# A two-layer encoder trunk on one core: how the fetched rows' sums are added, where the fetch dots stand, and the order of work at the layer border

## Chip, cores and metric

The kernel runs on one core of a Trainium2 chip, in one launch for both layers. The metric is the device time in microseconds (us); the median of three runs of the kernel before is 2080.5 us (2078.16 to 2082.45). One execution of it was also taken by the profiler: all rows below come from that one.

## What is computed

256 tokens of width 1024 go through two layers, float32 throughout. Cut to what matters here:

```python
def reference(x, ...):
    for layer in range(DEPTH):                      # DEPTH = 2
        h = rms_norm(x, norm1_g[layer])
        proj = h @ w_in[layer]                      # q, k, v of three mixers and the gate logits
        ya, yb, yc = diff_attention(...), chunk_band_attention(...), stick_breaking_attention(...)
        up = jnp.einsum('bsnw,nwd->bsnd', branches, w_branch[layer])
        x = x + jnp.sum(sigmoid(gl) * up, axis=2) @ w_out[layer]
        h2 = rms_norm(x, norm2_g[layer])
        x = x + peer(h2, peer_wq[layer], peer_subkeys[layer], peer_u[layer], peer_v[layer])
    return x

def peer(xn, wq, subkeys, u, v):                    # u, v: 16384 experts x 1024
    # per token and head (8 heads): the 16 best of 128 x 128 keys, softmax weights g over them
    hid = gelu(einsum('td,thkd->thk', x, u[expert]))
    return einsum('thk,thkd->td', g * hid, v[expert])
```

## The kernel before

Each engine has a program of its own and they meet at semaphores. TensorE multiplies float32 as three products of rounded parts (`w_hi`, `w_lo`). Every weight tile of 128 x 1024 comes by DMA into one of four slots of `raw` (SyncE's queue, line 431). ScalarE rounds it to `w_hi` (L1081 in the dense part, L1285 in the expert part); VectorE (L1437, L1886) or GpSimd (L570 in a loop, L552 written out) subtracts to give `w_lo`; the subtraction also frees the slot for the next DMA.

The experts of `peer` are done in two ways. For 224 tokens all 128 x 128 experts are computed densely, two tiles of 128 keys' rows at a time, called a pair: 64 pairs of `u` (24 "early" ones, then 40 in the fill stage), then 64 pairs of `v`. For the first 32 tokens (`SPARSE`) the 128 chosen rows per token are fetched by 64 indirect DMAs of 128 rows each from GpSimd (`gather`, L561): fetches 0 to 31 bring rows of `u`, 32 to 63 rows of `v`.

**The fill stage** (pairs u = 0 to 39). TensorE does two slots of 24 matmuls per pair (L605 to L607), and after a slot, one group of four matmuls that turns routing data of four tokens into weights (`gate_group`, L958). There are 56 groups in 40 pairs, so a pair has one group (after its second slot) or two (after each slot); `groups_of` sets it. Pairs 3, 5, 7, 9, 11, 13, 15, 17, 20, 22, 24, 26, 28, 30, 32, 34 and 36 have two, the last has none, the others one. VectorE takes each group in five steps (L1913, L1919, L1894, L1928, L1904), then multiplies the pair's hidden values (`weigh_fill`, L1937; its width is twice the tokens built so far, four per group). TensorE may begin pair u once `weigh_fill(u - 2)` is done. At ten pairs listed in `STEPS` VectorE then does the **dot** of one fetch (L1978, 128 x 1024, both inputs in SBUF); a fetch waits for the dot three before it (`g_taken`), since three buffers of `ring` take turns. In pair 38 VectorE also makes the weights of `v` pairs 0 and 1 (`weigh`: a copy, L1962, and a subtraction, L1966, each). GpSimd does the two `w_lo` splits of every fill pair and of `v` pairs 0 and 1, and issues a fetch behind the splits of the pair that stands two after its dot's:

```python
                for pair in range(PAIRS):
                    if pair < 2:
                        for e in range(2):
                            split_e(N_U + 2 * pair + e, 2 * pair + e)
                    while asked < GATHERS and STEPS[asked - RING] + 2 <= FILL + pair:
                        gather(asked)
```

**The v pairs.** TensorE does 32 matmuls a pair (L992, L994). Pair 0 ends with four chunks of output columns whose PSUM banks the fill stage used; they wait for `weigh_fill(39)`. VectorE's steps per pair are `weigh` (L1966), two splits (L1886) and a dot or, from pair 26 on, `add_rows` (L1996), which adds a fetched row to the running sums `xs`. The last of them is at pair 57. At pair 58 `add_sparse` adds the four partition groups of `xs` to `x`: one add, three copies into `ring`, three adds (L2004, L2006, L2009). VectorE works one pair ahead of TensorE.

**The layer border.** TensorE's last pair is split in four parts; ScalarE copies the low parts out (L1415), VectorE adds them (`turn`, L2054), TensorE transposes (`out_transposes`), VectorE adds to `x` (`add_experts`, L2063). Between them TensorE transposes `x` for the next layer (`norm_transposes`), VectorE multiplies the gains (L1446), ScalarE rounds to `hT_hi`, VectorE subtracts (L1454); ScalarE's first split of the new layer stands at the start of its loop body, and its two layers are one hardware loop.

## Time and profile before

| what | value |
|---|---|
| median of 3 runs | 2080.5 us |
| the profiled execution, its own time | 2079.86 us |
| its span, first to last instruction | 2078.1 us |
| mean granted TensorE clock | 0.997 of full |
| TensorE busy | 2038.3 us, 98% of the span |
| VectorE busy | 1662.9 us, 80% |
| ScalarE busy | 1236.8 us, 60% |
| GpSimd busy | 843.7 us, 41% |
| chain that ended last | TensorE 86%, VectorE 9%, ScalarE 2%, issue 2% |

The profiled execution lies 0.64 us under the median; 1.8 us of its time lie outside the span. Busy shares are means over the whole program; where TensorE stands still is read from its waits. Times in rows are us from the start of the span.

### The profile page before, as it was taken

What the parts mean: (1) busy time and instruction counts of PE and PEld (TensorE: products, weight loads), DVE (VectorE), ACT (ScalarE), POOL (GpSimd) and SP (SyncE); (2) the same over time, 40 slices, a digit from 0 to 9 for tenths busy, and PEclk for the clock granted to TensorE, in tenths of its full rate; (3) what the DMA queues carried; (4) which work ended last, traced back from release to release, by engine and by line L of the source; (5) the groups of instructions that cost most, each with busy time, mean ns of one, the idle gap of its engine ahead of it and who ended that gap; (6) DMA issues with size and microseconds to landing.
All of it is one profiled execution on the core that took longest, in us unless ns stands there. A gap on an engine that the chain in (4) does not pass through costs nothing.

```text
span 2078.1 us, 40819 instructions
## 1 busy us (share of the span) xinstructions
PE 2038.3 (98%) x14016; PEld 1878.2 (90%) x14016; DVE 1662.9 (80%) x2782; ACT 1236.8 (60%) x2036; POOL 843.7 (41%) x470
## 2 busy tenths in 40 slices
PE   8999999999999999999999999999999999999998
PEld 6777789999999999999877777899999999999997
DVE  5767877996899788788758678779978897878886
ACT  5855545458888645445468555454588885545443
POOL 2300005988788722122013000069888886222210
PEclk9999999999999999999999999999999999999999
DMA  6444554556565699899554445645565666998993
GB/s 239 142 153 142 191 185 151 195 199 213 184 203 193 203 314 316 291 314 318 187 196 153 151 142 183 202 150 195 194 213 192 201 196 219 315 307 295 319 309 136
DMA packets 122897, 446.85 MB, mean 215 GB/s; under 512 B 13968, under 2 KB 13968, under 8 KB 122256
## 3 DMA queue, kind: packets, MB, share of 16 engines
q1 hardware_dynamic: 102528, 371.24, 53.1%
q0 software_dynamic: 18432, 67.12, 10.0%
q10 hardware_dynamic: 1808, 6.89, 1.0%
q8 instruction: 67, 1.10, 0.2%
q14 instruction: 62, 0.51, 0.1%
HBM read 443.10 MB, written 1.05 MB: 214 GB/s over the span
## 4 chain that ended last, share of the span: by engine, by line
PE 86%; DVE 9%; ACT 2%; issue 2%; POOL 0%; DMA 0%; ACTq 0%; DVEq 0%; SPq 0%; POOLq 0%
PE ps L992 20%; PE ps L605 16%; PE ps L606 15%; PE ps L607 15%; PE ps L994 10%; PE ps L613 3%; PE ps L958 2%; PE ps L615 1%; PE ps L624 1%; DVE hot L1894 1%; DVE arena L1978 1%; DVE w_lo L1437 1%; DVE hot L1904 1%; PE ps L740 1%; PE ps L918 1%
## 5 line engine op out<-in xcount | busy, mean ns | idle before, releaser
L992 PE MATMUL ps<-wgt,w_hi 128*128 128x448 f32 x2048 | 645.8, 376 | 9.7 <-DVE w_lo L1886 5.9
L605 PE MATMUL ps<-hT,w_hi 128*128 128x224 f32 x2048 | 561.4, 274 | 5.1 <-DVE arena L1937 5.1
L607 PE MATMUL ps<-hT,w_lo 128*128 128x224 f32 x2048 | 561.4, 274 | 0.0
L606 PE MATMUL ps<-hT,w_hi 128*128 128x224 f32 x2048 | 561.4, 274 | 0.0
L994 PE MATMUL ps<-wgt,w_lo 128*128 128x224 f32 x2048 | 542.5, 265 | 0.0
L1285 ACT ACTIVATE w_hi<-raw 128x1024 fp32r<-128x1024 f32 x512 | 517.0, 1047 | 9.6 <-issue 3.2
L992 PEld LDWEIGHTS ps<-wgt,w_hi 128*128 128x128 f32 x2048 | 385.6, 188 | 40.5 <-DVE w_lo L1886 6.5
L552 POOL TENSOR_TENSOR w_lo<-raw,w_hi 128x1024 fp32r<-128x1024 f32 x168 | 400.1, 2404 | 46.9 <-ACT w_hi L1285 46.0
L605 PEld LDWEIGHTS ps<-hT,w_hi 128*128 128x128 f32 x2048 | 392.7, 192 | 6.8 <-DVE arena L1937 6.8
L607 PEld LDWEIGHTS ps<-hT,w_lo 128*128 128x128 f32 x2048 | 393.2, 192 | 0.0
L606 PEld LDWEIGHTS ps<-hT,w_hi 128*128 128x128 f32 x2048 | 392.8, 192 | 0.0
L994 PEld LDWEIGHTS ps<-wgt,w_lo 128*128 128x128 f32 x2048 | 392.3, 192 | 0.0
L1437 DVE TENSOR_TENSOR w_lo<-raw,w_hi 128x1024 fp32r<-128x1024 f32 x192 | 237.6, 1248 | 117.5 <-ACT w_hi L1081 117.2
L1886 DVE TENSOR_TENSOR w_lo<-raw,w_hi 128x1024 fp32r<-128x1024 f32 x248 | 292.7, 1221 | 38.2 <-ACT w_hi L1285 38.2
L570 POOL TENSOR_TENSOR w_lo<-raw,w_hi 128x1024 fp32r<-128x1024 f32 x96 | 230.8, 2424 | 113.3 <-ACT w_hi L1285 113.2
L1081 ACT ACTIVATE w_hi<-raw 128x1024 fp32r<-128x1024 f32 x192 | 200.9, 1057 | 122.5 <-PE ps L607 111.9
L1398 ACT ACTIVATE wgt<-arena 128x448 fp32r x124 | 71.8, 579 | 325.2 <-PE ps L994 325.0
L605 PE MATMUL ps<-w_hi,hT 128*128 128x512 f32 x480 | 197.0, 410 | 4.8 <-DVE hT L1454 3.5
L607 PE MATMUL ps<-w_hi,hT 128*128 128x512 f32 x480 | 189.5, 395 | 0.0
L606 PE MATMUL ps<-w_lo,hT 128*128 128x512 f32 x480 | 189.3, 394 | 0.0
L561 POOL DMA_INDIRECT arena<-in_w_v,route x64 | 73.9, 1155 | 267.0 <-DVE arena L1996 199.4
L1966 DVE TENSOR_TENSOR wgt<-arena,wgt 128x448 fp32r<-128x448 f32 x128 | 85.7, 670 | 83.8 <-ACT wgt L1398 83.6
(221 smaller groups left out, 3001.9 us busy)
## 6 DMA issues: line engine op xcount, KB each, us to landing
raw<-in_w_u SPq DMA_DIRECT2D x256, 512.0 KB, 3.3
raw<-in_w_v SPq DMA_DIRECT2D x256, 512.0 KB, 5.0
raw<-in_stream SPq DMA_DIRECT2D x192, 512.0 KB, 3.5
arena<-in_bias ACTq DMA_DIRECT2D x2, 1024.0 KB, 6.0
arena<-in_subk ACTq DMA_DIRECT2D x2, 1024.0 KB, 4.8
x<-in_x SPq DMA_DIRECT2D x4, 256.0 KB, 4.8
arena<-x ACTq DMA_DIRECT2D x8, 128.0 KB, 2.8
arena<-in_gain_rows ACTq DMA_DIRECT2D x2, 512.0 KB, 5.5
```

The source lines that it names most:

```text
L552: nc.gpsimd.tensor_tensor(w_lo[:, slot, :], raw[:, slot, :], w_hi[:, slot, :].bitcast(F), ALU.subtract).then_inc(early_ready.sem, 1)
L570: nc.gpsimd.tensor_tensor(w_lo[:, i, :], raw[:, i, :], w_hi[:, i, :].bitcast(F), ALU.subtract).then_inc(early_ready.sem, 1)
L605: mm(out_, left[0], right[0], start=start, stop=False, skip_group_check=group)
L606: mm(out_, left[0], right[1], start=False, stop=False, skip_group_check=group)
L607: return mm(out_, left[1], right[0], start=False, stop=stop, skip_group_check=group)
L992: mm(ps[:, c, 0:2 * DENSE], w_hi[:, 2 * k + e, dims], wgt[:, k, e, :, :].rearrange("p a b -> p (a b)"), start=first, stop=False, skip_grou ...
L994: return mm(ps[:, c, 0:DENSE], w_lo[:, 2 * k + e, dims], wgt[:, k, e, 0, :], start=False, stop=False, skip_group_check=True)
L1081: f(w_hi[:, n % SLOTS, :], raw[:, n % SLOTS, :], ACT.Copy).then_inc(hi_ready.sem, 1)
L1285: f(w_hi[:, slot, :], raw[:, slot, :], ACT.Copy).then_inc(hi_ready.sem, 1)
L1437: v.tensor_tensor(w_lo[:, i % SLOTS, :], raw[:, i % SLOTS, :], w_hi[:, i % SLOTS, :].bitcast(F), ALU.subtract).then_inc(w_ready.sem, 1)
L1886: v.tensor_tensor(w_lo[:, slot, :], raw[:, slot, :], w_hi[:, slot, :].bitcast(F), ALU.subtract).then_inc(w_ready.sem, 1)
L1966: v.tensor_tensor(wgt[:, k, :, 1, :], G[:, at:at + 2, :], wgt[:, k, :, 0, :].bitcast(F), ALU.subtract).then_inc(wgt_ready.sem, 1)
```

## The change

- `add_sparse` is gone. VectorE does one add of sums at each of v pairs 58, 59, 60 and 61 (`add_sums`); the three copies between partitions are ScalarE's now (`gather_sums`, at pairs 58, 59, 60, behind its splits), and VectorE waits for each by the new signal `sums_moved`. ScalarE's hardware loop over pairs ends at 56, and 56 to 63 are written out.
- The ten dots of the fill stage stand at pairs 8, 12, 16, 19, 23, 27, 31, 35, 37, 38 (before: 11, 14, 17, 20, 23, 26, 29, 32, 35, 38), all with one group. The fetches move with them, and the one that stood between GpSimd's splits of v pairs 0 and 1 stands behind those of pair 1 (`while pair and ...`).
- Border: TensorE does `out_transposes(1)` before the last part of the last pair, the transposes of `x` tiles 0 and 1 before `out_transposes(2)` and `(3)`, and in layer 1 those of tiles 2 and 3 after the first slot. VectorE does `add_experts(0)` before `turn(2)`, and the new layer's split and all steps of tiles 0 and 1 before `add_experts(1)`. ScalarE's split 0 of the new layer follows the second copy of low parts. SyncE's first four loads of layer 1 wait only for their own slots.
- ScalarE's two layers are written out.

```diff
 GATHERS = 2 * SPARSE
-STEPS = list(range(11, FILL - 1, 3))
+FILL_DOTS = (8, 12, 16, 19, 23, 27, 31, 35, 37, 38)
+STEPS = list(FILL_DOTS)
 STEPS += [FILL + 2 + i for i in range(SPARSE - len(STEPS))]
 STEPS += [FILL + FIRST_SUM + i for i in range(SPARSE)]
+LAST_SUM = STEPS[-1] - FILL
...
         wgt_hi = Signal(sem("wgt_hi"), PAIRS - 2)
+        sums_moved = Signal(sem("sums_moved"), PARTS - 1)
         diag_ready = Signal(sem("diag_ready"), 1)
...
             for layer in range(LAYERS):
-                def load_stream(r, k, first=False):
-                    load(layer, r * SLOTS + (min(k - 1, 0) if first else k + 1 - SLOTS), k,
+                def load_stream(r, k):
+                    load(layer, r * SLOTS + (k + 1 - SLOTS), k,
                          stream[bass.ds(r * SLOTS + (layer * N_STREAM + k), 1), :, :].rearrange("a p n -> p (a n)"))
                         load_x(2 * k + 1)
-                    if layer and k >= 2:
-                        sp.wait_ge(early_ready.sem, early_ready.at(layer, 0))
-                    load_stream(0, k, first=True)
+                    load_stream(0, k)
                 with sp.Fori(1, N_STREAM // SLOTS) as r:
...
                             split_e(N_U + 2 * pair + e, 2 * pair + e)
-                    while asked < GATHERS and STEPS[asked - RING] + 2 <= FILL + pair:
+                    while pair and asked < GATHERS and STEPS[asked - RING] + 2 <= FILL + pair:
                         gather(asked)
...
-                norm_transposes(lambda n: x_there(n, layer), (2,))
+                if layer == 0:
+                    norm_transposes(lambda n: x_there(n, layer), (2,))
...
                         if 4 * cb + k == 0:
-                            norm_transposes(lambda n: x_there(n, layer), (3,))
+                            norm_transposes(lambda n: x_there(n, layer), (3,) if layer == 0 else (2, 3))
...
                         out_transposes(0)
-                for n in range(1, 4):
+                        out_transposes(1)
+                if layer + 1 < LAYERS:
+                    x_there(1, layer + 1)
+                    norm_transposes(lambda n: x_there(n, layer + 1), (0, 1))
+                for n in range(2, 4):
                     out_transposes(n)
-                    if n == 2 and layer + 1 < LAYERS:
-                        x_there(1, layer + 1)
-                        norm_transposes(lambda n: x_there(n, layer + 1), (0, 1))
...
-            with act.Fori(0, LAYERS) as layer:
+            for layer in range(LAYERS):
                 def load_small():
...
-                def split(n):
+                def split(n, layer=layer):
...
-                split(0)
+                if layer == 0:
+                    split(0)
                 round_tiles(0, (0, 1))
...
                 f(hid, hid, ACT.Gelu, scale=scale_of).then_inc(hid_gelu.sem, 1)
-                with act.Fori(EARLY // 2, PAIRS // 2) as it:
+                def gather_sums(j):
+                    f(ring[j - 1][0:SPARSE, :], xs[j * SPARSE:(j + 1) * SPARSE, :], ACT.Copy).then_inc(sums_moved.sem, 1)
+                with act.Fori(EARLY // 2, LAST_SUM // 2) as it:
                     for k in range(2):
                         round_weights(it, k, 2 * k - 2 * EARLY)
+                for p in range(LAST_SUM // 2 * 2, PAIRS):
+                    round_weights(p // 2, p % 2, 2 * (p % 2) - 2 * EARLY)
+                    if p == LAST_SUM + 1:
+                        act.wait_ge(g_taken.sem, g_taken.at(layer, GATHERS))
+                        act.sem_inc(seen_act, 1)
+                    if 1 <= p - LAST_SUM < PARTS:
+                        gather_sums(p - LAST_SUM)
                 for n in range(4):
                       ).then_inc(v_lows.sem, 1)
+                    if n == 1 and layer + 1 < LAYERS:
+                        split(0, layer + 1)
                 act.wait_ge(act_chain, own.n)
...
-                def add_sparse():
-                    dve.wait_ge(g_taken.sem, g_taken.at(layer, GATHERS))
-                    dve.sem_inc(seen_dve, 1)
-                    own.one(v.tensor_tensor(x[0:SPARSE, 0, :], x[0:SPARSE, 0, :], xs[0:SPARSE, :], ALU.add).then_inc(dve_chain, 1))
-                    for j in range(1, PARTS):
-                        own.one(v.tensor_copy(ring[j - 1][0:SPARSE, :], xs[j * SPARSE:(j + 1) * SPARSE, :]).then_inc(dve_chain, 1))
-                    for j in range(1, PARTS):
+                def add_sums(j):
+                    part = xs[0:SPARSE, :]
+                    if j == 0:
+                        dve.wait_ge(g_taken.sem, g_taken.at(layer, GATHERS))
+                        dve.sem_inc(seen_dve, 1)
+                    else:
+                        dve.wait_ge(sums_moved.sem, sums_moved.at(layer, j))
                         dve.wait_ge(dve_chain, own.n)
-                        own.one(v.tensor_tensor(x[0:SPARSE, 0, :], x[0:SPARSE, 0, :], ring[j - 1][0:SPARSE, :], ALU.add
-                                                ).then_inc(dve_chain, 1))
-                    dve.wait_ge(dve_chain, own.n)
+                        part = ring[j - 1][0:SPARSE, :]
+                    own.one(v.tensor_tensor(x[0:SPARSE, 0, :], x[0:SPARSE, 0, :], part, ALU.add).then_inc(dve_chain, 1))
...
                             add_rows(q - SPARSE)
-                    if FILL + p == STEPS[-1] + 1:
-                        add_sparse()
+                    if 1 <= p - LAST_SUM <= PARTS:
+                        add_sums(p - LAST_SUM - 1)
                 dve.wait_ge(v_part.sem, v_part.at(layer, 1))
...
                 turn(1)
+                add_experts(0)
                 turn(2)
-                add_experts(0)
                 turn(3)
                 if layer + 1 < LAYERS:
-                    gain_tiles(0, (0,), layer + 1)
+                    split((0,), layer + 1)
+                    gain_tiles(0, (0, 1), layer + 1)
+                    rest_tiles(0, (0, 1), layer + 1)
                 add_experts(1)
-                if layer + 1 < LAYERS:
-                    gain_tiles(0, (1,), layer + 1)
-                    split((0,), layer + 1)
-                    rest_tiles(0, (0, 1), layer + 1)
                 dve.wait_ge(dve_chain, own.n)
```

Where the instructions stand, as each engine runs them, at three places that the rows below speak of.

GpSimd from the end of the fill stage to the fetches behind v pair 1. Each `L552` is one split, each `L561` one fetch; the four here are those of v pairs 0 and 1. Before:

```order
L550 REGISTER_ALU
L552 TENSOR_TENSOR w_lo<-raw,w_hi 128x1024 [waits hi_ready]
L550 REGISTER_ALU
L552 TENSOR_TENSOR w_lo<-raw,w_hi 128x1024 [waits hi_ready]
L559 REGISTER_ALU
L561 DMA arena<-in_u_rows,route 128x1024 [waits g_taken]
L550 REGISTER_ALU
L552 TENSOR_TENSOR w_lo<-raw,w_hi 128x1024 [waits hi_ready]
L550 REGISTER_ALU
L552 TENSOR_TENSOR w_lo<-raw,w_hi 128x1024 [waits hi_ready]
L559 REGISTER_ALU
L561 DMA arena<-in_u_rows,route 128x1024 [waits g_taken]
```

Now (the first row is the last split of u pair 39, the four behind the fetch are those of v pairs 0 and 1):

```order
L552 TENSOR_TENSOR w_lo<-raw,w_hi 128x1024 [waits hi_ready]
L559 REGISTER_ALU
L561 DMA arena<-in_u_rows,route 128x1024 [waits g_taken]
L550 REGISTER_ALU
L552 TENSOR_TENSOR w_lo<-raw,w_hi 128x1024 [waits hi_ready]
L550 REGISTER_ALU
L552 TENSOR_TENSOR w_lo<-raw,w_hi 128x1024 [waits hi_ready]
L550 REGISTER_ALU
L552 TENSOR_TENSOR w_lo<-raw,w_hi 128x1024 [waits hi_ready]
L550 REGISTER_ALU
L552 TENSOR_TENSOR w_lo<-raw,w_hi 128x1024 [waits hi_ready]
L559 REGISTER_ALU
```

The fetch between the two splits of v pair 0 and the two of v pair 1, which waits for the dot at u pair 38, is now behind all four. One fetch, which waits for the dot at u pair 37, stands right ahead of the four.

VectorE at the end of the fill stage, from the last step of u pair 37 to `weigh_fill(39)`. Before:

```order
L1928 TENSOR_TENSOR arena<-arena,ps 128x122x4
L1937 TENSOR_TENSOR arena<-arena,ps 128x2x220
L1913 TENSOR_TENSOR ps<-ps,low 128x4x124
L1919 TENSOR_TENSOR arena<-ps,low 128x4x4
L1928 TENSOR_TENSOR arena<-arena,ps 128x124x4
L1962 CAST wgt<-arena 128x2x224
L1966 TENSOR_TENSOR wgt<-arena,wgt 128x2x224
L1962 CAST wgt<-arena 128x2x224
L1966 TENSOR_TENSOR wgt<-arena,wgt 128x2x224
L1937 TENSOR_TENSOR arena<-arena,ps 128x448
L1978 SCALAR_TENSOR_TENSOR arena,qk_rs<-arena 128x1024
L1937 TENSOR_TENSOR arena<-arena,ps 128x448
```

Now (the same lines are 16 numbers further on):

```order
L1944 TENSOR_TENSOR arena<-arena,ps 128x122x4
L1953 TENSOR_TENSOR arena<-arena,ps 128x2x220
L1994 SCALAR_TENSOR_TENSOR arena,qk_rs<-arena 128x1024
L1929 TENSOR_TENSOR ps<-ps,low 128x4x124
L1935 TENSOR_TENSOR arena<-ps,low 128x4x4
L1944 TENSOR_TENSOR arena<-arena,ps 128x124x4
L1978 CAST wgt<-arena 128x2x224
L1982 TENSOR_TENSOR wgt<-arena,wgt 128x2x224
L1978 CAST wgt<-arena 128x2x224
L1982 TENSOR_TENSOR wgt<-arena,wgt 128x2x224
L1953 TENSOR_TENSOR arena<-arena,ps 128x448
L1994 SCALAR_TENSOR_TENSOR arena,qk_rs<-arena 128x1024
```

A dot (`L1994`) stands ahead of the steps of the last group; the two copies and subtractions for v pairs 0 and 1, `weigh_fill(38)`, the dot at 38 and `weigh_fill(39)` (one row further than shown) keep their order.

VectorE at the layer border, from its clearing of a buffer to the semaphore clear. Before:

```order
L2048 MEMSET arena 128x8x32
L2054 TENSOR_TENSOR arena<-ps,arena 128x2x224 x3
L2063 TENSOR_TENSOR x<-x,ps 128x512 x2
L2054 TENSOR_TENSOR arena<-ps,arena 128x2x224
L1446 TENSOR_TENSOR arena<-ps,gains 128x512
L2063 TENSOR_TENSOR x<-x,ps 128x512 x2
L1446 TENSOR_TENSOR arena<-ps,gains 128x512
L1437 TENSOR_TENSOR w_lo<-raw,w_hi 128x1024
L1454 TENSOR_TENSOR hT<-arena,hT 128x4x128 x2
L2079 ISA
```

Now:

```order
L2063 MEMSET arena 128x8x32
L2069 TENSOR_TENSOR arena<-ps,arena 128x2x224 x2
L2078 TENSOR_TENSOR x<-x,ps 128x512 x2
L2069 TENSOR_TENSOR arena<-ps,arena 128x2x224 x2
L1453 TENSOR_TENSOR w_lo<-raw,w_hi 128x1024
L1462 TENSOR_TENSOR arena<-ps,gains 128x512 x2
L1470 TENSOR_TENSOR hT<-arena,hT 128x4x128 x2
L2078 TENSOR_TENSOR x<-x,ps 128x512 x2
L2092 ISA
```

`turn` (`L2054`, now `L2069`) and `add_experts` (`L2063`, now `L2078`) alternate otherwise, and the split, the gains and the rests of tiles 0 and 1 stand ahead of the second `add_experts`.

## Rows read from the trace of the kernel before

**Rows 1.** Waits of TensorE, whole run: waited for, total us, times, longest us.
```profile
PE ps L992 <- DVE w_lo L1886: 5.9, 2, 3.0
...
PE ps L605 <- DVE arena L1937: 5.1, 8, 0.8
...
PE ps L605 <- DVE hT L1454: 3.5, 2, 2.5
PE ps L992 <- POOL w_lo L552: 3.2, 2, 1.6
```

**Rows 2.** Timeline of VectorE, layer 0, v pair 58: start, us, operation, [idle before].
```profile
1004.61 2.11 DVE L2006 COPY arena<-arena 32x1024 f32<-32x1024 f32 x3
1006.75 3.71 DVE L2009 TENSOR_TENSOR x<-x,arena 32x1024 f32<-32x1024 f32 x3
```

**Rows 3.** Timeline of ScalarE at v pairs 58 to 60 of layer 0.
```profile
1004.54 0.58 ACT L1398 ACTIVATE wgt<-arena 128x448 fp32r x1 [2.53 <-PE ps L994]
...
1009.56 0.58 ACT L1398 ACTIVATE wgt<-arena 128x448 fp32r x1 [2.54 <-PE ps L994]
...
1019.38 0.58 ACT L1398 ACTIVATE wgt<-arena 128x448 fp32r x1 [7.36 <-PE ps L994]
```

**Rows 4.** Timeline of ScalarE at the same place of layer 1.
```profile
2050.60 0.58 ACT L1398 ACTIVATE wgt<-arena 128x448 fp32r x1 [7.14 <-PE ps L994]
```

**Rows 5.** Stretch table: PE, PEld, DVE, ACT, POOL, SP busy (instructions), granted clock, DMA share, GB/s.
```profile
1012.30:1016.00 3.70, 3.69 (x13) 3.44 (x14) 3.70 (x4) 0.00 (x0) 0.00 (x0) 0.54 0.58 176
```

**Rows 6.** Timeline of VectorE in the fill stage of layer 0.
```profile
542.87 2.63 DVE L1978 SCALAR_TENSOR_TENSOR arena<-arena 128x1024 f32<-128x1024 f32 x1
...
557.69 0.48 DVE L1913 TENSOR_TENSOR ps<-ps,low 128x304 f32<-128x304 f32 x1 [2.57 <-ACT low L1371]
...
560.87 2.54 DVE L1978 SCALAR_TENSOR_TENSOR arena<-arena 128x1024 f32<-128x1024 f32 x1
```

**Rows 7.** Timeline of GpSimd there.
```profile
559.93 2.40 POOL L552 TENSOR_TENSOR w_lo<-raw,w_hi 128x1024 fp32r<-128x1024 f32 x1 [0.77 <-ACT w_hi L1285]
```

**Rows 8.** Timeline of TensorE at the start of u pair 17, layer 0.
```profile
569.59 0.37 PE L605 MATMUL ps<-hT,w_hi 128*128 128x224 f32 x1 [0.45 <-DVE arena L1937]
```

**Rows 9.** Timeline of GpSimd from u pair 38 to v pair 1, layer 0.
```profile
698.64 11.82 POOL L552 TENSOR_TENSOR w_lo<-raw,w_hi 128x1024 fp32r<-128x1024 f32 x5 [1.22 <-ACT w_hi L1285]
714.82 0.96 POOL L561 DMA_INDIRECT arena<-in_u_rows,route  x1 [4.36 <-DVE arena L1978]
715.81 4.73 POOL L552 TENSOR_TENSOR w_lo<-raw,w_hi 128x1024 fp32r<-128x1024 f32 x2
```

**Rows 10.** Timeline of VectorE in the same stretch.
```profile
701.73 0.61 DVE L1937 TENSOR_TENSOR arena<-arena,ps 128x440 f32<-128x440 f32 x1
706.50 0.68 DVE L1913 TENSOR_TENSOR ps<-ps,low 128x496 f32<-128x496 f32 x1 [4.17 <-ACT low L1371]
...
708.04 2.68 DVE L1962 CAST wgt<-arena 128x448 fp32r<-128x448 f32 x1
...
712.79 1.22 DVE L1978 SCALAR_TENSOR_TENSOR arena<-arena 128x1024 f32<-128x1024 f32 x1
...
717.57 3.46 DVE L1966 TENSOR_TENSOR wgt<-arena,wgt 128x448 fp32r<-128x448 f32 x1 [3.02 <-ACT wgt L1398]
```

**Rows 11.** Timeline of TensorE at the start of v pair 1.
```profile
718.33 0.44 PE L992 MATMUL ps<-wgt,w_hi 128*128 128x448 f32 x1 [1.61 <-POOL w_lo L552]
```

**Rows 12.** Timeline of all engines, earlier in layer 0, at a pair of GpSimd's splits.
```profile
457.32 4.90 POOL L570 TENSOR_TENSOR w_lo<-raw,w_hi 128x1024 fp32r<-128x1024 f32 x2 [0.81 <-ACT w_hi L1285]
...
457.53 4.73 DVE L1870 COPY route<-arena 32x32 f32<-32x32 f32 x2
```

**Rows 13.** Timeline of all engines at the layer border.
```profile
1042.82 1.28 ACT L1081 ACT_TABLE_LOAD   x1 [2.50 <-issue]
...
1047.18 0.76 PE L605 MATMUL ps<-w_hi,hT 128*128 128x512 f32 x1 [2.52 <-DVE hT L1454]
```

**Rows 14.** Timeline of TensorE at the end of the program.
```profile
2073.33 0.66 PE L624 MATMUL ps<-ident,arena 128*128 128x128 f32 x4 [1.59 <-DVE arena L2054]
```

## Prediction

> **What bounds the kernel.** I read the waits of TensorE first, then the timelines of VectorE, ScalarE and GpSimd around the largest of them. TensorE is busy nearly throughout (98% in the table above), so only what it waits, and what it runs at a low clock behind a wait, can be won. The list of its waits names what the change aims at [rows 1]: two stops of 3.0 us for VectorE's splits of `v` tiles (5.9 in all), eight of up to 0.8 us in the fill stage for `weigh_fill` (5.1), two for the first rests at the border and start (3.5), two of 1.6 us for GpSimd's splits at v pair 1 (3.2). In each layer the places are the same, so most terms count twice.
>
> **The sums.** VectorE does three copies (2.11 us) and three adds (3.71) in one piece at pair 58, with one more add ahead of them [rows 2]. ScalarE's copy of a pair's low weights shows TensorE's beat: 1009.56 behind 1004.54 is 5.02 us a pair, with 2.54 us idle on ScalarE; the next one stands 9.82 us on, with 7.36 idle, and in layer 1 7.14 [rows 3, 4]. So a layer loses 7.36 - 2.54 = 4.82, the other 7.14 - 2.54 = 4.60. TensorE's own stop is 3.0 of that; the rest, some 1.7, is the slow clock behind it: granted 0.54 of full, that is the 1.2 GHz level, over the stretch after the stop [rows 5]. Spread out, a pair asks of VectorE one subtraction for the weights (about 0.6), two splits (about 2.4) and one add of 3.71 / 3 = 1.24: 4.2 of 5.02 us, less than TensorE takes. ScalarE's copies (at most as long as VectorE's 0.70; say 1.0) fall into its 2.54 us of idle. A new wait (`sums_moved`) is met one pair early. **-9.4 us** (between -7 and -9.4, if a tight pair costs half a microsecond in each of four).
>
> **The dots of the fill stage.** A dot with the port free takes 1.22 us [rows 10]. Here it takes 2.63 and 2.54: at 560.87 GpSimd is in a split that runs from 559.93 to 562.33, and the dot ends at 563.41, 1.08 us behind it [rows 6, 7]. So the dot waits for the split and then runs. By the Trainium skill, page "SBUF — State Buffer", section "Who interferes with whom", a VectorE operation with two SBUF inputs and a GpSimd operation that reads SBUF take the same port pair, whole instruction by whole instruction; the dot's row agrees.
>
> Does it hurt? VectorE has a cushion of 2.57 us behind a one-group pair [rows 6], and none behind a two-group pair. The dot at 14 (one group) is followed by pair 15, with two groups in which VectorE catches up on nothing; `weigh_fill(15)` comes late and TensorE stops 0.45 us before pair 17 [rows 8]. The eight stops of [rows 1] are four a layer, of 0.45 to 0.80, each behind a two-group pair that follows a dot at a one-group pair (14, 23, 29, 35). The dots that stand **at** two-group pairs (11, 17, 20, 26, 32), as the one at 542.87, cause none: the next pair has one group and its cushion takes them. The change does the reverse of what this asks: the dots at 8, 12, 16, 19, 23, 27, 31 and 35 stand at one-group pairs, each with a two-group pair right behind. Eight stops a layer of 0.35 (early, where the width is small) to 0.80 come to 4.6 against 5.1 / 2 = 2.55: +2.0 a layer, **+4.1 us** (between -5.1, if such a dot costs nothing there, and +5.5).
>
> **The start of the v pairs.** Before, the fetch between GpSimd's splits waits for the dot at 38: GpSimd stands still 4.36 us, from 710.46 to 714.82, and TensorE waits 1.61 at v pair 1 [rows 9, 11]. The change takes that wait away (-1.61 a layer). But those 4.36 us were VectorE's: in them it did all that stands in the order between the first `CAST` and the dot. The copy at 708.04 took 2.68 us, to 0.26 behind the end of GpSimd's five splits; the dot followed at 712.79 [rows 9, 10]. `weigh_fill(39)` came 0.1 after the dot, at 714.0, when nobody waited for it.
>
> Now four splits stand together, 4.73 for two, 2.37 each [rows 9]. On the same time axis: `weigh_fill(37)` ends at 702.34 [rows 10]; the new dot waits for the split that ends near 703.4, runs to 704.5 and delays the last split of the fill stage to 706.9; the fetch (0.96) puts the first v split near 708.1. VectorE's last group ends at 707.9 (start 706.50 and three steps, the copy at 708.04) [rows 10]. From here both want the port at every step. The trace has such a case: two VectorE copies of 32 x 32 take 4.73 us beside two splits of 4.90, one passing at the end of each split [rows 12]. I take that: copy 708.0, split, subtraction, split, copy, split, subtraction, split, each VectorE step of 0.3 to 0.6 also holding GpSimd up. Four splits of 2.37 and 2.0 of VectorE bring it to 719.6; the dot ends at 720.8 and `weigh_fill(39)` (0.6, its input in PSUM) at 721.3. The last four chunks of v pair 0 wait for exactly this; they are 4 of its 16 products of a chunk, a quarter of 5.02 us or 1.25, so v pair 1 begins at 722.6 instead of 718.33: +4.2 a layer. TensorE then stood some 5.8 us instead of 1.6; I add the 1.7 of slow clock that the stops of 3 us in the sums cost. 5.9 a layer, **+11.8 us** (between -3.2, the wait gone and nothing in its place, and +16).
>
> **Border and end.** The table load of 1.28 goes from ScalarE's way; TensorE's first slot of layer 1 began at 1047.18 behind a stop of 2.52 [rows 13]. It should begin near 1044.6, but tiles 2 and 3 are now transposed behind slot 0 and VectorE's rests and gains for them hold up its split for slot 1, which gives back about 1.8. With what the transposes move, **-0.6** (-2.5 to +1). The end: `add_experts(0)` ahead of `turn(2)` shortens the last stops, of which one of 1.59 shows [rows 14]: **-0.7** (-1.2 to +0.3). SyncE's freed waits and the rest: 0, hidden under TensorE's slots.
>
> **Sum.** -9.4 + 4.1 + 11.8 - 0.6 - 0.7 = +5.2. On the profiled execution's 2079.86 that is 2085.1; the median lies 0.64 higher, so **2085.7 us**. A measurement of this kernel tells about 0.2% (4.2 us) from no change: 2076.3 to 2084.7 is "same".
>
> **Rivals.**
> - *VectorE keeps the port once it has it* (ends faster). GpSimd reads a register and waits on a semaphore between two splits (order rows); VectorE's next step waits for nothing. If copy, subtraction, copy, subtraction and dot pass in one go behind a split, as they did from 710.46 in GpSimd's gap, they cost at most 2.37 and 4.36 behind 707.9: 714.6, ahead of 715.5, when TensorE comes to the last four chunks (718.33 - 1.61 - 1.25). That is the point from which it decides: one split waited for is free, each more costs 2.4. Then the v start gives -3.2 to 0: sum -9.8 to -6.6, **2070.7 to 2074**. For it: nothing in the order forces one for one. Against it: [rows 12].
> - *The dots are harmless too* (the change does what its tables say). -9.4 - 5.1 - 3.2 - 1.3 = -19.0: **2061.5**. Against it stands the pattern of the eight stops.
> - *VectorE is passed over.* The subtraction at 717.57 took 3.46: it began inside a split of a pair that ran to 720.54 and ended at 721.03, so it did not pass at the end of the first [rows 9, 10]. If the copy waits for all four splits (to 717.5) and the 4.36 follow, `weigh_fill(39)` ends at 722 to 723, and the slow clock lasts longer: 1 to 2 more a layer, **2087 to 2090**. By the rule of the Trainium skill cited above ("SBUF — State Buffer", "Who interferes with whom"), each instruction takes and gives back the ports, which speaks for the forecast's path; this row disagrees.
>
> **Chances.** Forecast 0.50 (its own range 2081 to 2089), port kept 0.28, all harmless 0.08, passed over 0.12, other 0.02. Range 2070 to 2090: it takes in three of the four. Faster: 0.28 + 0.08 + 0.02 of the forecast's low end = 0.38. Slower: 0.29 of the forecast (above 2084.7) and 0.12 = 0.41. Same: 0.21.
>
> **What would show it.** In the profile after: TensorE's waits for VectorE's splits of `v` gone, and ScalarE's idle at pair 60 back to 2.5; 14 to 16 waits for `weigh_fill` in the fill stage, the new ones behind pairs 9, 13, 17, 20, 24, 28, 32 and 36; a stop of 4 to 6 us at the last chunks of v pair 0, with `weigh_fill(39)` as what ends it, and GpSimd's four splits stretched to over 11 us; no table load at the border. Wrong would be: `weigh_fill(39)` done by 715.5 on this axis, or no new waits in the fill stage.

## The result, and the profile after

| what | before | changed |
|---|---|---|
| median of the runs | 2080.8 us (2078.16 to 2082.45, 4 runs) | 2093.92 us (2092.57 to 2094.95, 4 runs) |
| span of the profiled execution | 2078.1 us | 2091.4 us |
| mean granted TensorE clock | 0.997 | 0.994 |

The changed kernel is slower: ratio 1.0061, 95% interval 1.0048 to 1.0074, +13.1 us. Forecast were 2085.7 us (+5.2) and a range of 2070 to 2090.

Waits of TensorE, changed kernel, whole run; they answer to [rows 1]:

```profile
PE ps L993 <- issue: 13.9, 2, 7.0
PE ps L605 <- DVE arena L1953: 9.2, 16, 0.8
...
PE ps L605 <- DVE hT L1470: 5.0, 2, 2.6
PE ps L605 <- DVE w_lo L1453: 2.6, 4, 1.5
PE ps L624 <- ACT arena L1136: 0.8, 1, 0.8
```

The stops for VectorE's splits of `v` tiles and for GpSimd's splits are gone. There are 16 waits for `weigh_fill` instead of 8, and two new stops of 7 us. GpSimd there, answering to [rows 9]:

```profile
708.61 0.95 POOL L561 DMA_INDIRECT arena<-in_u_rows,route  x1
709.57 9.31 POOL L552 TENSOR_TENSOR w_lo<-raw,w_hi 128x1024 fp32r<-128x1024 f32 x4
723.24 0.96 POOL L561 DMA_INDIRECT arena<-in_u_rows,route  x1 [4.36 <-DVE arena L1994]
```

VectorE in the same stretch, answering to [rows 10]:

```profile
703.46 0.60 DVE L1953 TENSOR_TENSOR arena<-arena,ps 128x440 f32<-128x440 f32 x1
703.99 2.23 DVE L1994 SCALAR_TENSOR_TENSOR arena<-arena 128x1024 f32<-128x1024 f32 x1
...
709.78 9.36 DVE L1978 CAST wgt<-arena 128x448 fp32r<-128x448 f32 x1
719.17 0.63 DVE L1982 TENSOR_TENSOR wgt<-arena,wgt 128x448 fp32r<-128x448 f32 x1
...
722.35 0.62 DVE L1953 TENSOR_TENSOR arena<-arena,ps 128x448 f32<-128x448 f32 x1
```

The first copy for the `v` weights waits for the end of all four splits, 709.57 + 9.31 = 718.88. What comes behind it (0.6, 0.4, 0.6) shows that the copy itself is short. TensorE has no weights for v pair 0:

```profile
719.90 0.71 PE L993 MATMUL ps<-wgt,w_hi 128*128 128x448 f32 x1 [6.97 <-issue]
```

and then runs at a granted clock of 0.51, the lower of its two levels, 1.2 GHz. The stretch table (PE, PEld, DVE, ACT, POOL busy, granted clock, DMA share, GB/s), in which TensorE gets through 18 matmuls of the pair's 32 in 5.30 us:

```profile
719.90:725.20 5.30, 5.30 (x18) 4.91 (x19) 3.03 (x6) 0.00 (x0) 0.96 (x1) 0.51 0.41 114
```

**Where the time went.** The same instruction of both traces, held against each other place by place (changed minus before, us):

| stretch | layer 0 | layer 1 |
|---|---|---|
| up to the fill stage (layer 1: the border with its dense part) | -1.4 | +3.9 |
| fill stage, to `weigh_fill(37)` | +3.1 | +3.1 |
| start of the v pairs | +7.3 | +7.3 |
| the sums | -4.9 | -4.6 |
| the end of the program | | -0.6 |

Together +13.2; the spans differ by 13.3. For instance `weigh_fill(37)` begins at 703.46 instead of 701.73, +1.7, and ScalarE's fourth copy of the v pairs at 742.82 instead of 733.82, +9.0: the start of the v pairs cost 7.3.

### The profile page after: what moved, and what is told of

The parts are those of the page before. It is cut to its first block, busy times and chain, and to the rows that moved or that the text cites. A ratio compares the mean times of both kernels' runs of the same rounds, so it can differ in the third digit from the quotient of the medians.

```text
span 2091.4 us, 40220 instructions
## 1 busy us (share of the span) xinstructions
PE 2039.7 (98%) x14016; PEld 1878.4 (90%) x14016; DVE 1663.8 (80%) x2776; ACT 1240.7 (59%) x2042; POOL 845.1 (40%) x470
## 3 DMA queue, kind: packets, MB, share of 16 engines
HBM read 443.10 MB, written 1.05 MB: 212 GB/s over the span
## 4 chain that ended last, share of the span: by engine, by line
PE 81%; DVE 12%; issue 3%; ACT 2%; DMA 1%; POOL 0%; DVEq 0%; SPq 0%; POOLq 0%; ACTq 0%
PE ps L993 21%; PE ps L605 14%; PE ps L607 14%; PE ps L606 14%; PE ps L995 10%; PE ps L613 3%; DVE hot L1910 3%; DVE arena L1994 2%; DVE hot L1920 1%; PE ps L615 1%; PE ps L624 1%; DVE ps L1929 1%; DVE w_lo L1453 1%; PE ps L959 1%; DVE arena L1935 1%
## 5 line engine op out<-in xcount | busy, mean ns | idle before, releaser
L552 POOL TENSOR_TENSOR w_lo<-raw,w_hi 128x1024 fp32r<-128x1024 f32 x168 | 402.0, 2414 | 58.5 <-ACT w_hi L1288 57.1
L1401 ACT ACTIVATE wgt<-arena 128x448 fp32r (+1 forms) x124 | 71.7, 578 | 323.5 <-PE ps L995 323.2
L561 POOL DMA_INDIRECT arena<-in_w_v,route x64 | 73.1, 1142 | 267.8 <-DVE arena L2012 200.1
L1361 ACT ACTIVATE hot<-hot,route_hi 128x128 fp32r<-128x128 f32 x448 | 142.9, 393 | 24.9 <-DVE hot L1920 24.3
```

The costliest lines, as they stand in the source:

```text
L552: nc.gpsimd.tensor_tensor(w_lo[:, slot, :], raw[:, slot, :], w_hi[:, slot, :].bitcast(F), ALU.subtract).then_inc(early_ready.sem, 1)
L1361: last = f(row, row.bitcast(F), ACT.Copy, scale=route_hi[:, SPARSE + 4 * n + q:SPARSE + 4 * n + q + 1].bitcast(F))
```

## Experiments

Fourteen kernels; ratios are to runs of the kernel before on the same chip. Unless said, a diff is against the changed kernel. One kernel's runs spread over 2 to 9 us, and the traces show part of why: two stops (1.9 us each, at about 100 and 1140 us) and the slow clock behind some stops are there in one execution and missing in another. So each verdict rests on rows too.

### Undoing the two placements

```diff
-                    while pair and asked < GATHERS and STEPS[asked - RING] + 2 <= FILL + pair:
+                    while asked < GATHERS and STEPS[asked - RING] + 2 <= FILL + pair:
```

> Changed kernel, but the fetch that waits for the dot at 38 stands again between GpSimd's splits of v pair 0 and those of v pair 1. In the changed kernel VectorE's first copy for the v weights took 9.36 us, until all four splits were done. Theory P (VectorE is passed over as long as GpSimd's next split is ready, and gets the port when GpSimd has to wait): the copy is held over two splits, 4.5 to 5 us, TensorE's stop before v pair 0 falls from 6.97 to about 2.3 us, and v pair 1 starts some 4.5 us earlier per layer: 2093.9 - 9 = about 2085 (2082 to 2088). Rival A (the copy is slow for a reason of its own, such as the dot at 37 right ahead of it): the copy stays at 9 us and the time at 2092 to 2096.

Measured: 2084.1 us, ratio 1.0005 (0.9995 to 1.0015). The copy took 4.80 us and the stop before v pair 0 2.41, as theory P said. The wait of 1.6 us for GpSimd's split was back in layer 0; layer 1 has none.

```diff
-FILL_DOTS = (8, 12, 16, 19, 23, 27, 31, 35, 37, 38)
+FILL_DOTS = tuple(range(11, FILL - 1, 3))
```

> Changed kernel with the ten dots of the fill stage at 11, 14, ..., 38 again; the fetch stays behind all four splits. Both theories: the waits for weigh_fill fall from 16 (9.2 us) to 8 (5.1 us), and the fill stage gives back about 3.1 us per layer, what it grew by. Theory P: no fetch and no dot break GpSimd's row of splits, so the copy is held again, from 708 to about 715 on the axis of before (7 us), TensorE stops about 4.5 us at v pair 0: v start +4.5 per layer against before where the changed kernel had +7.3. Sum: 2093.9 - 6.2 - 5.6 = 2082 (2079 to 2086). Rival A (the dot at 37 makes the long copy): the copy takes 2.7 us or less, the v start costs nothing: 2093.9 - 6.2 - 14.6 = 2073.

Measured: 2076.04 us, ratio 0.9971 (0.9962 to 0.9981). The fill stage's waits fell to 8 (5.1 us). Theory P is out: the copy was not held over the row. Rival A had the copy right (2.67 us) and the time nearly (2073 of 2080.8 is 0.9963), but the v start was not free: TensorE stopped 2.3 us in each layer before v pair 0. GpSimd, then VectorE's two copies and the first subtraction:

```profile
699.38 17.03 POOL L552 TENSOR_TENSOR w_lo<-raw,w_hi 128x1024 fp32r<-128x1024 f32 x7 [1.23 <-ACT w_hi L1288]
```

```profile
708.78 2.67 DVE L1978 CAST wgt<-arena 128x448 fp32r<-128x448 f32 x1
711.49 2.67 DVE L1982 TENSOR_TENSOR wgt<-arena,wgt 128x448 fp32r<-128x448 f32 x1
714.08 2.58 DVE L1978 CAST wgt<-arena 128x448 fp32r<-128x448 f32 x1
```

Each step waits for one split: the one-for-one passage that the prediction had assumed, in a row of seven splits. So a long row alone does not shut VectorE out. What does, the dot at 37 (rival A) or the fetch that comes with it, this run leaves open; e13 and e14 below decide it.

> Changed kernel with both undone: dots at 11, 14, ..., 38 and the fetch between the splits. What is left is the sums, the border and ScalarE's written-out layers. If the stages add up as the two traces show (fill +3.1 and v start +7.3 per layer are gone): 2093.9 - 20.8 = 2073.1 (2071 to 2075), with the copy at 2.7 us, 8 waits for weigh_fill and 1.6 us of wait at v pair 1 per layer. Rival (the placements interact with the border, or the stages don't add): off that by more than 2 us.

Both edits together: 2072.68 us, ratio 0.9958 (0.9944 to 0.9972). The medians lie 10.7 us apart (before's is 2083.41 on that chip), the ratio says 8.7. Expected were 2073.1 where before has 2080.8, 7.7 below; within the interval. The copy took 2.68 us again, and the waits of the fill stage (5.1 us, 8 times) and for GpSimd's splits (3.2 us, twice) were those of [rows 1].

### Is it the wait that opens a window?

```diff
+                    if pair == 1:
+                        pool.wait_ge(wgt_ready.sem, wgt_ready.at(layer, 2))
                     if pair < 2:
                         for e in range(2):
                             split_e(N_U + 2 * pair + e, 2 * pair + e)
```

> Changed kernel with one wait more: GpSimd waits for the weights of v pairs 0 and 1 before its splits of v pair 1. No instruction is moved. Theory P: the wait is a window in which VectorE does copy, subtraction, copy, subtraction in one go behind the second split (copy 4.5 to 5 us instead of 9.36); TensorE's stop before v pair 0 falls to 2.3 us; the dot at 38 is then held over the last two splits and weigh_fill(39) with it, a second stop of about 2 us before the last chunks of v pair 0. Net 3 us per layer: 2093.9 - 6 = 2088 (2085 to 2090). Rival B (a wait on GpSimd frees nothing, what counts is that it issues a DMA there): the copy stays at 9 us, and the added wait makes it slower: over 2096.

Measured: 2083.09 us, ratio 1.0000 (0.9990 to 1.0010), a larger gain than was expected (2088 of 2080.8 is 1.0035). The copy took 4.80 us, the stops were 2.41 and 1.29. A wait of GpSimd does what the fetch's did in the kernel before; rival B is out.

```diff
+        idle_tile = sb("idle_tile", [P, 4])
...
                         for e in range(2):
+                            if pair or e:
+                                own.one(nc.gpsimd.memset(idle_tile[:, 2 * pair + e:2 * pair + e + 1], 0.0).then_inc(pool_chain, 1))
                             split_e(N_U + 2 * pair + e, 2 * pair + e)
```

> Changed kernel with a tiny GpSimd instruction (memset 128x1, reads nothing from SBUF) between each two of the four splits. Theory Q (GpSimd's next instruction is already waiting when the split ends, and it keeps VectorE out as long as its signals came early): nothing changes, the copy for the v weights stays at 9 us or more, time as the changed kernel's, 1.006 of before. Rival R (VectorE gets in wherever two splits are not adjacent): the copy takes 2.7 us or less, and the stop of 7 us before v pair 0 falls to 1 us or less.

Measured: 2094.58 us (one run). GpSimd, then VectorE:

```profile
711.71 2.40 POOL L553 TENSOR_TENSOR w_lo<-raw,w_hi 128x1024 fp32r<-128x1024 f32 x1
714.04 0.10 POOL L590 MEMSET idle_tile<- 128x1 f32 x1
714.10 2.36 POOL L553 TENSOR_TENSOR w_lo<-raw,w_hi 128x1024 fp32r<-128x1024 f32 x1
```

```profile
711.88 9.47 DVE L1981 CAST wgt<-arena 128x448 fp32r<-128x448 f32 x1
```

Rival R is out: an instruction that waits for nothing opens no window.

```diff
-                def split_e(n, slot):
-                    pool.wait_ge(hi_ready.sem, hi_ready.at(layer, N_STREAM + n + 1))
+                def split_e(n, slot, later=0):
+                    pool.wait_ge(hi_ready.sem, hi_ready.at(layer, N_STREAM + n + 1 + later))
...
-                            split_e(N_U + 2 * pair + e, 2 * pair + e)
+                            split_e(N_U + 2 * pair + e, 2 * pair + e, int(2 * pair + e < SLOTS - 1))
```

> Changed kernel where GpSimd's first three v splits wait for one rounding of ScalarE more than they need, so that the signal on which the second and third wait comes 0.6 and 0.2 us before the split ahead ends (in the changed kernel 2.7 and 2.9 us before). Nothing else moves. Theory Q (VectorE gets the port at a split's end if the next split's signal came late, less than a microsecond before; it is passed over if it came 2 us or more before): the copy takes some 2.5 us instead of 9.36, the first subtraction passes at the next end, TensorE's stop before v pair 0 falls from 6.97 to about 2.3 us; the second copy is held over the last split. Net 2 to 3 us per layer: ratio to before 1.003 to 1.004. Rival (VectorE is always passed over in a row of splits): copy 9 us, 1.006 or above.

Measured: 2092.58 us, ratio 1.0053 (1.0035 to 1.0071); the interval just reaches the 1.003 to 1.004 of theory Q. The profiled execution is the fastest of the four, 2088.14 us. GpSimd, then VectorE:

```profile
711.26 4.73 POOL L552 TENSOR_TENSOR w_lo<-raw,w_hi 128x1024 fp32r<-128x1024 f32 x2
716.30 5.36 POOL L552 TENSOR_TENSOR w_lo<-raw,w_hi 128x1024 fp32r<-128x1024 f32 x2 [0.32 <-ACT w_hi L1288]
```

```profile
711.45 4.80 DVE L1978 CAST wgt<-arena 128x448 fp32r<-128x448 f32 x1
716.28 0.63 DVE L1982 TENSOR_TENSOR wgt<-arena,wgt 128x448 fp32r<-128x448 f32 x1
716.83 2.60 DVE L1978 CAST wgt<-arena 128x448 fp32r<-128x448 f32 x1
```

The rows decide, and theory Q fell in both directions. The second split's signal came at 713.02, 0.6 us before the first one ended, and the copy did not pass. The last split's signal had come at 716.13, 2.5 us before the end at which the second copy did pass (the last two splits took 5.36 instead of 4.73: VectorE was in between). Behind the first real wait (0.32 us) the passage is one for one again.

### The fetch right ahead of the row

What the rows with no passage have in common, here, in e1, e4, e11 and in [rows 9, 10] at 717.57, is a fetch right ahead. e2 had none.

```diff
-                    while pair > 4 and asked < GATHERS and STEPS[asked - RING] + 2 <= pair:
+                    while 4 < pair < FILL - 1 and asked < GATHERS and STEPS[asked - RING] + 2 <= pair:
```

> Changed kernel with the fetch that waits for the dot at 37 behind GpSimd's four v splits instead of right ahead of them; all dots stay. Theory F (a row of splits right behind a fetch is not let go for VectorE until its end; a row without a fetch ahead of it lets VectorE in at each end): the copy takes 2.7 us or less instead of 9.36 and each later step waits for one split at most; TensorE's first stop falls from 7 to 1 to 2.5 us, a second one of 3 to 4.5 us comes at the last chunks of v pair 0. 3 to 4 us less per layer than the changed kernel: ratio to before 1.002 to 1.0035. Rival G (the dot at 37 close ahead, or the instant at which the copy asks, 0.2 us behind a split's start, makes it wait): the copy stays at 4.8 to 9.4 us, 1.005 or above.

Measured: 2086.14 us, ratio 1.0024 (1.0011 to 1.0038) against the changed kernel's 1.0061; TensorE's stops were 1.0 and 3.5 us, as theory F said. GpSimd, then VectorE:

```profile
699.02 18.16 POOL L552 TENSOR_TENSOR w_lo<-raw,w_hi 128x1024 fp32r<-128x1024 f32 x7 [1.22 <-ACT w_hi L1288]
717.33 1.16 POOL L561 DMA_INDIRECT arena<-in_u_rows,route  x1
```

```profile
708.42 1.29 DVE L1978 CAST wgt<-arena 128x448 fp32r<-128x448 f32 x1
709.75 2.69 DVE L1982 TENSOR_TENSOR wgt<-arena,wgt 128x448 fp32r<-128x448 f32 x1
712.36 2.58 DVE L1978 CAST wgt<-arena 128x448 fp32r<-128x448 f32 x1
714.97 2.69 DVE L1982 TENSOR_TENSOR wgt<-arena,wgt 128x448 fp32r<-128x448 f32 x1
```

And the converse, on e2_dots_back:

```diff
-                    while pair > 4 and asked < GATHERS and STEPS[asked - RING] + 2 <= pair:
+                    while pair > 4 and asked < GATHERS and STEPS[asked - RING] + 2 <= pair and (asked != 11 or pair == FILL - 1):
```

> e2_dots_back (dots at 11, 14, ..., 38, no dot at 37, copy held over one split, ratio 0.9971) with one fetch, the one that waits for the dot at 35, put right ahead of the four v splits. Theory F: the copy is held to the end of the fourth split, 8 to 9.5 us, TensorE's stop before v pair 0 grows from 2.3 to about 6 us, v pair 1 is 3.5 to 5 us later per layer: ratio 1.0005 to 1.002. Rival G: no dot at 37 and another instant at which the copy asks, so the copy stays at 2.7 us and the ratio at 0.997 to 0.998.

Measured: 2084.61 us, ratio 1.0010 (0.9998 to 1.0023), against 0.9971. GpSimd, then VectorE:

```profile
702.94 0.96 POOL L561 DMA_INDIRECT arena<-in_u_rows,route  x1 [0.16 <-issue]
703.92 9.33 POOL L552 TENSOR_TENSOR w_lo<-raw,w_hi 128x1024 fp32r<-128x1024 f32 x4
```

```profile
705.08 8.43 DVE L1978 CAST wgt<-arena 128x448 fp32r<-128x448 f32 x1
```

The copy asked 1.2 us into the first split, no dot stood near, and it waited for all four; TensorE's stops were 6.0 us. Theory F holds in both directions, and rival G is out. In this kernel the dot at 37 did its harm by bringing its fetch to the place ahead of the four splits.

The other rows agree. In the traces of all sixteen kernels, over the fill stages and the starts of the v pairs of both layers, one can look for a copy, subtraction or dot of VectorE with its operands in SBUF that asks while GpSimd still has another split of the row to begin. Behind a fetch there are 22 such cases, and all 22 wait for the row's end; in rows that begin behind a wait of GpSimd there are 32, and all 32 get in before it. A wait ahead of the fetch does not help: in [rows 9] it is 4.36 us long, and the subtraction at 717.57 was held even so. Why a fetch has this effect is not shown.

### The parts alone, and the best of them

On the kernel before, the change's hunks for `add_sums`, `gather_sums` and `sums_moved` and nothing else:

```diff
-                def add_sparse():
+                def add_sums(j):
...
+                    if 1 <= p - LAST_SUM < PARTS:
+                        gather_sums(p - LAST_SUM)
```

> The kernel before with the sums' change alone (adds over four pairs, ScalarE's copies, pairs 56 to 63 written out); layers in ScalarE's loop, border, dots and fetch as before. The two traces showed 4.9 and 4.6 us gained at this place. Expected: before - 9.5 us (-8.5 to -10.5), ratio about 0.9954; no table load moved, no stop for VectorE's splits of v tiles. Rival: if the border and the written-out layers of the changed kernel are what gained, this one gains less than 7 us.

Measured: 2070.39 us, ratio 0.9930 (0.9914 to 0.9947). That is a gain of 14.4 us (11 to 18 by the interval), more than was expected; the profiled spans, 2068.5 against 2078.1, give 9.6, and e3_both_back, which has the same sums, 10.7. The stops for VectorE's splits of `v` tiles are gone and the rest of TensorE's list of waits is that of before, so the place is settled and the last 2 to 5 us of the size are not.

On e3_both_back:

```diff
-FILL_DOTS = tuple(range(11, FILL - 1, 3))
+FILL_DOTS = (9, 13, 17, 20, 24, 28, 32, 34, 36, 38)
```

> e3_both_back with the ten dots at 9, 13, 17, 20, 24, 28, 32, 34, 36 (all pairs with two groups, each followed by one with one group) and 38. Theory (a dot is harmless where the next pair has one group): the eight waits for weigh_fill (5.1 us) are gone, and with what slow clock and refill stand behind them the time falls by 5 to 7 us: ratio to before 0.993 where e3_both_back has 0.9958. Rival (what counts is that VectorE is more loaded in a two-group pair): the waits are at other pairs, 8 or more of them, and the time is that of e3_both_back or above.

Measured: 2070.24 us, ratio 0.9936 (0.9919 to 0.9953), with the interval of e3_both_back (0.9958) overlapping. No wait for `weigh_fill` is left in the list. At the start of the v pairs stand:

```profile
PE ps L993 <- issue: 4.6, 2, 2.3
...
PE ps L993 <- POOL w_lo L552: 1.6, 1, 1.6
```

The theory of the dots holds. Part of the gain is given back, in both layers: the dot at 36 brings its fetch (in layer 0 at 696.74) ahead of a row of four splits (697.72 to 707.14), two of pair 39 and two of v pair 0. The copy asked at 702.51 and took 4.89 us, to the row's end, and TensorE stopped 2.3 us. It is theory F's pattern again.

Also on e3_both_back:

```diff
+        warm = sb("warm", [P, 1])
...
+            f(warm[:], half_neg[:, 0:1], ACT.Exp)
             for layer in range(LAYERS):
...
+                if layer + 1 < LAYERS:
+                    f(warm[:], half_neg[:, 0:1], ACT.Exp)
                 act.wait_ge(act_chain, own.n)
```

> e3_both_back with two tiny exponentials (128x1) on ScalarE: one before its first wait for a weight tile, one behind the last copy of the low parts at the border. Writing out the layers moved the load of the function table from ScalarE's idle time at the start (2.43, beside a DMA) to 7.26, behind that DMA, and in layer 1 from the border to 1060, in the middle of the stream of tiles. Theory (the moved table loads cost what the border change lost): slot 0 of layer 0 begins 1.8 us earlier, the state at 87 us 0.7 to 1 us earlier; in layer 1 the waits behind 1060 (0.8 to 1.0 for ScalarE's eviction and 0.3 for a split) go: 1.5 to 2.5 us less than e3_both_back in all. Rival (the transposes of tiles 2 and 3 behind slot 0 are the whole loss): no change beyond 0.7 us.

The loads in the changed kernel stand here (ScalarE):

```profile
7.26 1.28 ACT L1083 ACT_TABLE_LOAD   x1 [7.26 <-DMA raw<-in_stream]
...
1060.06 1.28 ACT L1121 ACT_TABLE_LOAD   x1
```

and in this one here:

```profile
1.44 1.28 ACT L1059 ACT_TABLE_LOAD   x1 [1.44 <-PEq L2168]
...
1036.19 1.28 ACT L1436 ACT_TABLE_LOAD   x1
```

Measured: 2070.94 us, ratio 0.9935 (0.9917 to 0.9953), too near e3_both_back's 0.9958 for the medians. The stages tell more. The wait at 87 us stands at 87.08, against 88.53 in e3_both_back and 87.74 in the changed kernel. In all sixteen traces it stands at 86.65 to 87.40 where the load is early (five) and at 87.74 to 88.77 where it is behind the DMA wait (eleven), so the load's new place at the start costs TensorE time. From the second slot of layer 1 to the wait 70 us on it takes 71.3 us as in the kernel before, where the changed kernel and e3_both_back take 73.1 and 73.3. That looks like the second load's price, but e9_all_together below speaks against it.

> e3_both_back with the tenth dot behind pair 39 (behind weigh_fill(39)) instead of 38, the fetch that waits for it behind all four splits, and GpSimd's wait for the weights of v pairs 0 and 1 before its splits of v pair 1. Dots at 11, 14, ..., 35, 39. Theory P with its window: copy, subtraction, copy, subtraction pass in one go, the splits of pair 1 begin right then, 3.4 us earlier than before, the dot is held over them and nobody waits for it. The 1.6 us of wait at v pair 1 go: 3.2 to 4 us less than e3_both_back, ratio 0.9940. Rival: the held dot makes weigh(2) and the splits of pair 2 late, TensorE stops at v pair 2 for 1 us or more per layer and nothing is won.

On e3_both_back, with the wait of e4_window:

```diff
-FILL_DOTS = tuple(range(11, FILL - 1, 3))
+FILL_DOTS = tuple(range(11, 36, 3)) + (39,)
```

Measured: 2068.36 us, ratio 0.9918 (0.9902 to 0.9935), a larger gain than the expected 0.9940. GpSimd's splits no longer stand in TensorE's waits, and nothing has come in their place.

> All that has paid, on the changed kernel: sums and border of the change; ten dots at 11, 13, 17, 20, 22, 26, 28, 32, 34 (two-group pairs) and 39; GpSimd's wait for the weights of v pairs 0 and 1 ahead of its splits of pair 1, the fetch behind them; the two tiny exponentials that put the table loads back. If the parts add: sums -9.5, fill -5 to -6, v start -3.2 to -4, border and end -1 to -2 against before: before - 20 us (-17 to -23), ratio 0.9904. No waits for weigh_fill, none for GpSimd's splits. Rival (parts take from each other, as the wait for GpSimd's split came back in e6_two_group_dots): before - 14 or less.

> The same dots, wait and sums on the kernel before, with its border order and ScalarE's layers in a loop. Expected: sums -9.5, fill -5 to -6, v start -3.2 to -4: before - 19 us, ratio 0.9909. If the border's new order is worth something once the table loads are back, e9_all_together is 1 to 2 us below this one; if not, they are equal.

In both, with the wait of e4_window, on e7_tables and on e5_sums_only:

```diff
+FILL_DOTS = (11, 13, 17, 20, 22, 26, 28, 32, 34, 39)
```

Measured: 2061.0 us, ratio 0.9895 (0.9878 to 0.9913), and 2062.38, ratio 0.9901 (0.9883 to 0.9919). VectorE in the first of them:

```profile
704.90 2.27 DVE L1984 CAST wgt<-arena 128x448 fp32r<-128x448 f32 x1
707.20 0.62 DVE L1988 TENSOR_TENSOR wgt<-arena,wgt 128x448 fp32r<-128x448 f32 x1
...
709.77 2.77 DVE L2000 SCALAR_TENSOR_TENSOR arena<-arena 128x1024 f32<-128x1024 f32 x1
```

The parts add: some 21 us below before, 33 below the changed kernel by the medians. With or without the border's order cannot be told apart. Both beat both kernels.

The trace of e9_all_together also corrects the reading of e7_tables. Its second table load is at the border again (1030.57), yet the stretch from the second slot of layer 1 to the wait 70 us on takes 73.35 us. TensorE stops behind a copy of ScalarE, and ScalarE waits for the DMA of a weight tile. TensorE and ScalarE in the changed kernel:

```profile
1070.53 1.24 PE L624 MATMUL ps<-ident,arena 128*128 128x128 f32 x8 [0.82 <-ACT arena L1136]
1068.84 1.06 ACT L1083 ACTIVATE w_hi<-raw 128x1024 fp32r<-128x1024 f32 x1 [4.43 <-DMA raw<-in_stream]
```

and in e9_all_together:

```profile
1054.81 1.24 PE L627 MATMUL ps<-ident,arena 128*128 128x128 f32 x8 [1.07 <-ACT arena L1140]
1053.12 1.06 ACT L1087 ACTIVATE w_hi<-raw 128x1024 fp32r<-128x1024 f32 x1 [5.67 <-DMA raw<-in_stream]
```

Of the thirteen kernels with the changed border twelve take 72.6 to 73.7 us for this stretch, whether the load is moved or not, and only e7_tables takes 71.3; the three with the old border take 71.3 to 71.4. So the loss goes with the changed border and a weight tile that lands late, and the table load is not shown to cause it. In e9_all_together against e10_without_border the two sides cancel: the second slot comes 1.9 us earlier behind ScalarE's first low-part copy (14.44 against 16.33), and the stretch behind it is 2.0 longer (73.35 against 71.34).

## Why the prediction failed

The sign was right and so were the places where time was won and lost; the size was not, and the range ended 4 us too low. Between forecast (+5.2) and traces (+13.2) lie 8.0 us: 2.8 at the start of the v pairs, 2.1 in the fill stage and 3.1 from the border and the dense parts.

- **The sums, -9.4: right.** -4.9 and -4.6. ScalarE in the changed kernel, answering to [rows 3]:

```profile
1008.44 0.58 ACT L1401 ACTIVATE wgt<-arena 128x448 fp32r<-128x448 f32 x1 [2.54 <-PE ps L995]
1010.94 1.06 ACT L1413 ACTIVATE arena<-arena 32x1024 f32<-32x1024 f32 x1
1013.45 0.58 ACT L1401 ACTIVATE wgt<-arena 128x448 fp32r<-128x448 f32 x1 [1.46 <-PE ps L995]
```

  Its copy of 1.06 comes out of the 2.54 us of idle time, and TensorE keeps its 5.01 us a pair.
- **The dots, +4.1: mechanism right, size short.** The idle time in the list rose by just 9.2 - 5.1 = 4.1 us and at the pairs named. But the stages grew by 6.2. TensorE's own rows, held against those of before, show the price of a stop: behind an idle of 0.37 us it stood 0.63 later, behind 0.44 us 0.70, behind 0.73 us 1.00. Each stop costs its idle time and 0.26 to 0.28 us more. Four stops more a layer make 1.05 us, 2.1 in all, which is what 4.1 lacks. The term that was mis-sized is the price of a stop: 0.35 to 0.80 was taken from the waits alone.
- **The start of the v pairs, +11.8: the step that failed** is "I take that: copy 708.0, split, subtraction, split, copy, split, subtraction, split". That path is real (e2, e13), but not here. Two of the prediction's own signs say so: the four splits were to stretch to over 11 us and took 9.31, and the stop was to come at the last chunks of v pair 0 and came before its first. The rival "VectorE is passed over", given 0.12, is what happened, and it had the evidence: the subtraction at 717.57 was in a row of splits right behind a fetch; the copies of [rows 12] were not. It was read as an exception. The copy waited for four splits, `weigh_fill(39)` ended at 722.97 (1.73 less on the axis of before: 721.2; the forecast said 721.3), yet the cost was 7.3 instead of 5.9 a layer. That the instant came out right is luck: another path led to it. What was mis-sized is where TensorE stood: with the first copy late it stopped before the whole of v pair 0, 6.97 us, and ran more than half of that pair at half clock, while the forecast let it do three quarters of the pair first. In e13_fetch_behind, where VectorE does pass one for one, the same stage costs 4.2 a layer (ScalarE's fourth copy 36.24 behind `weigh_fill(37)`, before 32.09), so the forecast's 5.9 was also too high for its own path. The rule of the Trainium skill cited in the prediction (page "SBUF — State Buffer", section "Who interferes with whom") has each instruction take and give back the ports; e2 and e13 agree with 2.6 to 2.7 us per step, the changed kernel's 9.36 and e14's 8.43 do not, and the measurement decides.
- **The border, -0.6: wrong, by what was put at nothing.** Slot 0 came 2.5 us earlier against ScalarE's first low-part copy (9.10 instead of 11.60) and slot 1 stopped 1.48, so that it stood where it had stood (16.03 against 16.11): as forecast. But the prediction looked at the table load at the border alone. With the layers written out it also moved at the program's start, behind the wait for the first tile: +0.7 at 87 us. And "SyncE's freed waits and the rest: 0" does not hold for the dense part of layer 1, where TensorE lost 1.7 us behind a weight tile that landed late (see e9_all_together). The second table load, now at 1060.06 in the stream of tiles, may have a share in it; which part of the border's change makes the tile late stays open. Another 2.1 us of layer 1's +3.9 is a stop of 1.9 us that this execution had and the one of before had not (the list of waits, before and changed, has 3 and 4 stops of this kind); in layer 0 the +0.7 of the table load was outweighed by 1.6 us less behind the stop at 100 us, where this execution's clock stayed up (granted 1.00 over the next 5 us, before 0.72 and 0.61), and by 0.5 us that no row explains.

```profile
PE ps L711 <- DVE arena L1565: 3.9, 3, 1.9
PE ps L712 <- DVE arena L1581: 5.7, 4, 1.9
```

- **The end, -0.7: right**, -0.6.

The range failed since it stopped at rival three's bounds for that place and left no room for the price per stop, for the moved table load and for the late tile.

## What to carry to other kernels

Before a wait is moved away, look at who works in its shadow: in GpSimd's 4.36 us of waiting VectorE did four steps and the dot in one go, and a deliberate wait in the right place was worth more than the wait's removal. When a trace shows two readings of one contention (one passage per split, and none), find what differs ahead of the two rows before choosing, and price the start of a stage for the first instruction that is late, not the last. Writing out a hardware loop also moves what a compiler puts at its head, such as ScalarE's table loads. And a stage that is shorter in one execution does not show the cause yet: here a second kernel with the same cure had the loss again.

## What the runs showed of the hardware

- A row of GpSimd subtractions (128x1024, 2.33 to 2.37 us each) lets a waiting VectorE operation with SBUF operands in at the end of each (2.58 to 2.69 us a step), except behind an indirect DMA of GpSimd: there the operation waited for the whole row, 9.36, 8.43, 9.47 us for four and 4.80 for two. This held in all 22 cases behind a fetch and in all 32 others. A small instruction in between (0.10 us) changes nothing; a wait of GpSimd on a signal not yet there, even 0.32 us, does.
- A stop of TensorE in the fill stage (idle 0.37 to 0.73 us) costs its idle time and 0.26 to 0.28 us more.
- After the same stop of 2.4 us at the border TensorE's first to twelfth matmul took 2.6 us in five executions (e2, e4, e6, e7, e9) and 3.8 to 4.2 in eight (the changed kernel, e1, e3, e8, e11, e12, e13, e14). Over the next 2.9 us the granted clock was 1.00 in e7 and 0.59 in the changed kernel: whether the clock falls to the lower level behind such a stop differs from execution to execution.
